# Retention in two transformer layers: one 512-token score triangle against four chunks of 128 with a running state

## The chip, the cores and the metric

One core of a Trainium2 chip runs one program. The metric is the device time of the execution in microseconds. Before the change it is 2685.18 us, median of 3 runs (2685.07 to 2685.32).

## The reference, cut to what matters

The program computes two layers of a three-branch mixer with a feed-forward part, and then one layer of a second kind of block with attention. There are 512 tokens of width 1024, all in float32. The change touches the retention branch of the first two layers, which has 4 heads of 128 dimensions:

```python
log_g = jnp.log(1.0 - 2.0 ** (-5.0 - jnp.arange(h)))
q, k = rotary(q), rotary(k);  q = q * (dk ** -0.5)
def step(state, inp):                       # by chunks of CHUNK tokens
    s = einsum('bhid,bhjd->bhij', qi, ki) * decay_mask     # g^(i-j), i >= j
    intra = einsum('bhij,bhjv->bhiv', s, vi)
    inter = einsum('bhid,bhdv->bhiv', qi * q_decay, state)
    new_state = state * chunk_decay + einsum('bhjd,bhjv->bhdv', ki * k_decay, vi)
    return new_state, intra + inter
y_b = head_norm(out, ret_gn_w, center=True) * silu(rg)
```

Without the chunks this is: output i is the sum over all j up to i of g^(i-j) (q_i . k_j) v_j. Any size of chunk gives the same result.

## The kernel before, in words

Every tensor lies with its channels on the partitions and its 512 tokens along the free dimension; only the values `r_v` have tokens on the partitions, in four tiles of 128. A projection (`pe_block`, lines 504 to 506) multiplies a block of 1024 weight columns with the activations. Weights and activations are split into a high and a low part in a faster format (`w_hi`, `w_lo`), and three products are summed. Weight blocks come by DMA into `raw`; ScalarE makes the high part (line 686), VectorE the low part (line 690), into a ring of four slots. Each engine has its program written out by hand, in one order, and waits on semaphores. The `split(i)` calls stand where block i + 3 is split.

In the stretch around the change TensorE computes the projections GR to GR + 3 (the gates of the other branch), one for each retention head h. Behind projection GR + h stand `ret_scores(h)` (lines 1786 to 1797), `ret_out(h - 1)` (1799 to 1810) and, from h = 2 on, the variance product of a head, `head_var`. The scores are the lower triangle in tiles of 128 keys: key tile 0 with 512 queries, tile 1 with 384, tile 2 with 256, tile 3 with 128, so 1280 columns, in ordinary float32. VectorE multiplies them with the mask g^(i-j) (`ret_decay`, line 2572) into `s_ret`, and TensorE multiplies the values with them, again 1280 columns.

PSUM has eight banks of 512 columns. Banks 0 to 3 take the projections; banks 4 to 7 are given out in a fixed order by `side_banks`. A `Use` of a bank has two semaphores: `filled` (TensorE is done) and `drained` (its reader is done); the next user waits for the one before to be drained. Scores of a head use banks 4, 5 and 6, outputs 7, variances 6.

VectorE's order for head h is: `square_low` (h of 2 and up), the low split of a weight block, `gate_in` (line 2564, projection result times the root), `ret_decay`, `gated` (line 2570). ScalarE's is: the high split of a weight block, `gate_silu` (line 2121), then for the output of the head before a copy, a square and its high part (lines 2070, 2073, 2077), and from h = 2 on a change of the activation table and two steps of the root (lines 2084, 2087).

Of the kernel before, what the change touches and what calls it, by code (L numbers as in the profile page):

```python
# [26 lines left out]
ALU = mybir.AluOpType  # L27
# [17 lines left out]
LEVELS = (1, 128, 64, 32, 16, 8, 4, 2, 256, 512)  # L45
MASKED = LEVELS[1:8]
HALF = P // 2
Q_IN = 6
Q_S = 4
TH = T // 2  # L50
# [55 lines left out]
N_PAR = P_WGA + KD * RANK  # L106

H_FIRST, H_F1POST, H_MPRE, H_MPOST, H_F2PRE, H_F2POST, H_QN, H_KN = 0, 8, 16, 24, 32, 40, 48, 49
N_PAR2 = 50

C_ONES, C_IDENT, C_BD64 = range(3)
N_SQ = 3
# [70 lines left out]
def side_banks():  # L183


    layer = [("pre0", 7), ("tm0", 6), ("ga", 4), ("z0", 7), ("z1", 6)]
    layer += [(key, 4 + i % 4) for i, key in enumerate(k for n in range(len(LEVELS)) for k in level_keys(n))]
    layer += [("out0", 7), ("out1", 7), ("out2", 7), ("var0", 6), ("out3", 7), ("var1", 6), ("var2", 6), ("var3", 6)]
    for h in range(HEADS):
        layer += [(f"s{h}0", 4), (f"s{h}1", 5), (f"s{h}2", 6)]  # L190
        if h >= 1:
            layer += [(f"out{3 + h}", 7)]
        if h >= 2:
            layer += [(f"var{2 + h}", 6)]
    layer += [("out7", 7), ("var6", 6), ("var7", 6), ("post0a", 7), ("post0b", 7), ("pre1", 7), ("post1a", 7), ("post1b", 7)]
    second = [("pre2", 7), ("post2a", 7), ("post2b", 7), ("pre3", 7), ("tm3", 4), ("vt", 4)]
    second += [(f"qvar{i}", 6) for i in range(5)]
    second += [(f"dv{t}", 4 + t) for t in range(TT)]
    second += [(f"pt{u}", 4 + u % 2) for u in range(64)] + [(f"o{g}", 6 + g % 2) for g in range(KD)]
    second += [("post3a", 7), ("post3b", 7), ("pre4", 7), ("post4a", 7), ("post4b", 7)]  # L200
    table, used = {}, [0] * 8
    for key, b in layer:
        table[key] = (b, used[b])
        used[b] += 1
    per = list(used)
    used = [LAYERS * n for n in per]
    for key, b in second:
        table[key] = (b, used[b])
        used[b] += 1
    return table, per  # L210


def build(nc, dram):
    ctx = ExitStack()
    with ctx:
# [35 lines left out]
        row_sum = place("row_sum", [P, 4])  # L251
        row_inv = place("row_inv", [P, 4])
        wait_cell = place("wait_cell", [P, 40])
        ones_r = place("ones_r", [P, P], F32R)
        sq_hi_at = top[0]
        sq_hi = place("sq_hi", [P, 2, T], F32R)
# [44 lines left out]
        s_ret = region("s_ret", [P, 2, 1280], 16)  # L301
# [114 lines left out]
        rot_moved = [sem(f"rot_moved{i}") for i in range(2)]  # L416
        rv_sum = ev("rv_sum", 4)
        rv_cent = ev("rv_cent", 4)
        hn_sq = ev("hn_sq", 8)
        hn_hi = ev("hn_hi", 8)  # L420
        hn_lo = ev("hn_lo", 8)
# [1301 lines left out]
        def _(pe):  # L1723
# [61 lines left out]

            def ret_scores(h, li):
                pe.wait_ge(rot_y.sem, rot_y.upto(li, 4 + h + 1))
                use = side(f"s{h}0", li)
                pe.wait_ge(use.drained, use.n + 1)
                nc.tensor.matmul(use.mem[:, :], r_k[:, h, tok(0)], r_q[:, h, :], start=True, stop=True).then_inc(use.filled, 1)  # L1790
                use = side(f"s{h}1", li)
                pe.wait_ge(use.drained, use.n + 1)
                nc.tensor.matmul(use.mem[:, 0:384], r_k[:, h, tok(1)], r_q[:, h, tok(1, 3)], start=True, stop=True)
                nc.tensor.matmul(use.mem[:, 384:512], r_k[:, h, tok(3)], r_q[:, h, tok(3)], start=True, stop=True).then_inc(use.filled, 1)
                use = side(f"s{h}2", li)
                pe.wait_ge(use.drained, use.n + 1)
                nc.tensor.matmul(use.mem[:, 0:256], r_k[:, h, tok(2)], r_q[:, h, tok(2, 2)], start=True, stop=True).then_inc(use.filled, 1)

            def ret_out(h, li):
                for i in range(3):  # L1800
                    src = side(f"s{h}{i}", li)
                    pe.wait_ge(src.drained, src.n + 2)
                if h == 0:
                    pe.wait_ge(rv_cent.sem, rv_cent.upto(li, 4))
                use = side(f"out{4 + h}", li)
                pe.wait_ge(use.drained, use.n + 1)
                s = s_ret[:, h % 2, :]
                for kt, a, b in ((0, 0, 512), (1, 512, 896), (2, 896, 1152), (3, 1152, 1280)):
                    mm = nc.tensor.matmul(use.mem[:, tok(kt, TT - kt)], r_v[:, kt, tok(h)], s[:, a:b], start=kt == 0, stop=kt == 3)  # L1809
                mm.then_inc(use.filled, 1)  # L1810

            def head_var(n, li):
# [7 lines left out]
            def layer(li):  # L1820
# [38 lines left out]
                pe_values(pe, bl, RV, ou, RV)  # L1859
                for h in range(HEADS):  # L1860
                    project(GR + h)
                    ret_scores(h, li)
                    if h >= 1:
                        ret_out(h - 1, li)
                    if h >= 2:
                        head_var(2 + h, li)
                project(RG)
                ret_out(3, li)
                project(RG + 1)
# [6 lines left out]
                for t in range(GATE_ST):  # L1876
                    o = gate_outs(og, t)
                    for i in range(GATE_BLOCKS):
# [3 lines left out]
                        if i >= O_FIRST:  # L1882
# [4 lines left out]
                            for tile in range(2):  # L1887
                                n = 2 * st + tile
                                if t > 0:
                                    pe.wait_ge(branch_free[n].sem, branch_free[n].upto(li, t))  # L1890
                                else:
                                    src = side((f"s{HEADS - 1}0", f"s{HEADS - 1}1", "var7", "out7")[n], li)
# [169 lines left out]
        def _(act):  # L2062
# [56 lines left out]
            def gate_silu(g, ou, li):  # L2119
                act.wait_ge(drained[ou.bank(GR + g)], ou.uses(GR + g) + 2)  # L2120
                nc.scalar.activation(tgate[g % 2][:, :], tgate[g % 2][:, :], ACT.Silu).then_inc(silu_g.sem, 1)

            def y_high(n, li):

                if n < 4:
# [15 lines left out]
            def layer(li):  # L2141
# [67 lines left out]
                values(bl, RV, ou, RV, r_v, li, 1)  # L2209
                for h in range(HEADS):  # L2210
                    split(GR + h)
                    gate_silu(h, ou, li)
                    if h >= 1:
                        head_copy(3 + h, li)
# [29 lines left out]
                    act.wait_ge(block_done, bg.n(p) + 1)  # L2244
                    nc.scalar.activation(w_hi[:, bg.slot(p), :], gate_weights(bg, li, t, i), ACT.Copy).then_inc(hi_split, 1)

                src = side(f"s{HEADS - 1}2", li)
                act.wait_ge(src.filled, src.n + 1)
                mixed_high(G_T4)
                mixed_high(G_Z)  # L2250
                split(RG)
# [204 lines left out]
        def _(dve):  # L2456
# [115 lines left out]
            def ret_decay(h, li):  # L2572
# [6 lines left out]
                    dve.wait_ge(old.filled, old.n + 1)  # L2579
                use = side(f"s{h}0", li)  # L2580
                dve.wait_ge(use.filled, use.n + 1)
                nc.vector.tensor_tensor(s[:, 0:512], use.mem[:, :], mask, ALU.mult).then_inc(use.drained, 1)
                use = side(f"s{h}1", li)
                dve.wait_ge(use.filled, use.n + 1)
                nc.vector.tensor_tensor(s[:, 512:896], use.mem[:, 0:384], mask[:, 0:384], ALU.mult)
                nc.vector.tensor_tensor(s[:, 1152:1280], use.mem[:, 384:512], mask[:, 0:128], ALU.mult).then_inc(use.drained, 1)
                use = side(f"s{h}2", li)
                dve.wait_ge(use.filled, use.n + 1)
                nc.vector.tensor_tensor(s[:, 896:1152], use.mem[:, 0:256], mask[:, 0:256], ALU.mult).then_inc(use.drained, 1)

            def layer(li):
                bl, ou, s = layer_blocks(li), layer_outs(li), li * 2
# [102 lines left out]
                for h in range(HEADS):  # L2695
                    if h >= 2:
                        square_low(2 + h, li)
                    split(GR + h)
                    gate_in(h, bl, ou, li)
                    ret_decay(h, li)  # L2700
                    gated(h, li)
                    if h == 3:
# [129 lines left out]
                def merged_low(k):  # L2832
                    dve.wait_ge(mg_hi_ev.sem, mg_hi_ev.upto(li, k + 1))
                    nc.vector.tensor_tensor(mg_lo[:, k, :], mg_f[:, k, :], mg_hi[:, k, :].bitcast(F32), ALU.subtract).then_inc(mg_lo_ev.sem, 1)

                square_low(6, li)
                head_norm(5, li)
                mixed_low(G_T4)
# [291 lines left out]
    return v.reshape(-1, P).T  # L3130


def layer_parameters(a):
    out = []
    for li in range(LAYERS):
# [9 lines left out]
def second_gains(a):  # L3145
    cols = [per_partition(a["norm_mix_pre"][0])]
    cols += [per_partition(a[n + "_2"][0]) for n in ("ffn1_post_g", "mix_pre_g", "mix_post_g", "ffn2_pre_g", "ffn2_post_g")]
    cols += [np.concatenate([a[n + "_2"][0][AXIAL]] * 2).reshape(P, 1) for n in ("q_norm_g", "k_norm_g")]
    return np.concatenate(cols, axis=1)


def constants():
# [9 lines left out]
    c = np.arange(T)[None, :] - np.arange(P)[:, None]  # L3162
    log_g = np.log(1.0 - 2.0 ** (-5.0 - np.arange(HEADS)))
    decay = [np.where(c >= 0, np.exp(lg * np.maximum(c, 0)), 0.0).astype(f) for lg in log_g]
    inv = np.power(f(10000.0), -np.arange(HD, dtype=f) / f(HD)).astype(f)

    t = np.arange(T)
# [42 lines left out]
```

## Time and profile before

| | |
|---|---|
| median of 3 runs | 2685.18 us |
| the profiled execution's own time | 2685.19 us |
| its span, from first to last instruction | 2683.4 us |
| TensorE busy | 2668.1 us |
| VectorE busy | 1915.7 us |
| ScalarE busy | 1323.4 us |
| granted TensorE clock, mean | 0.999 |

The busy times overlap. TensorE's products are pipelined: the duration of one reaches past the start of the next, so the distance from start to start, which the chain of waits gives, is what a product costs in a series. The retention of the first layer lies at 224 to 265 us of the span, that of the second at 1082 to 1123 us.

### The profile page before, as it was taken

Reading aid. Unit: us, or ns where it says so; the run is one execution under the profiler, and the core shown is the slowest. Engines: PE = TensorE matmul, PEld = TensorE weight load, DVE = VectorE, ACT = ScalarE, POOL = GpSimd, SP = SyncE. Lnnn points to the kernel's source line nnn. Section 1 sums busy time; section 2 is a strip of 40 time slices with the busy share of each in tenths; the row PEclk is TensorE's granted clock in tenths of the full one; section 3 lists DMA queues with packets and bytes.
Section 4 is the critical chain, followed back from the end, with each engine's and each line's share of the span. In section 5 each row is a group of like instructions: output and inputs, shape, how many; then the busy total and the mean of one; then the engine's idle time right before and its main releaser. Section 6 shows DMA issues by size and latency. Waiting matters only on the chain.

```text
span 2683.4 us, 41896 instructions
## 1 busy us (share of the span) xinstructions
PE 2668.1 (99%) x17044; PEld 2391.4 (89%) x17044; DVE 1915.7 (71%) x2703; ACT 1323.4 (49%) x1984; POOL 57.0 (2%) x59
## 2 busy tenths in 40 slices
PE   9999999999999999999999999999999999999998
PEld 7887999899988888799989998999988877899987
DVE  6946877688854785687678883588854798688843
ACT  5344644555542534554465562455542467455631
POOL 0020000000000003000000000000000000000000
PEclk9999999999999999999999999999999999999999
DMA  4242332333333324133333333233332430233232
GB/s 150 79 126 65 117 102 79 118 118 100 98 108 89 110 83 130 55 118 106 114 100 107 103 93 104 80 118 99 99 107 90 118 107 2 72 118 111 93 103 80
DMA packets 77216, 266.23 MB, mean 99 GB/s; under 512 B 9600, under 2 KB 12032, under 8 KB 76128
## 3 DMA queue, kind: packets, MB, share of 16 engines
q1 hardware_dynamic: 71136, 254.86, 30.6%
q10 hardware_dynamic: 5888, 8.68, 1.2%
q8 instruction: 136, 2.23, 0.3%
q14 instruction: 56, 0.46, 0.1%
HBM read 251.71 MB, written 4.19 MB: 95 GB/s over the span
## 4 chain that ended last, share of the span: by engine, by line
PE 96%; DVE 2%; ACT 1%; issue 0%; DMA 0%; ACTq 0%; DVEq 0%; SPq 0%
PE bank L504 29%; PE bank L505 29%; PE bank L506 29%; PE bank L2035 1%; PE bank L2013 1%; PE bank L1762 1%; PE bank L1999 1%; PE bank L1778 1%; PE bank L1809 1%; DVE w_lo L690 0%; DVE x L856 0%; DVE u_lo L788 0%; ACT w_hi L686 0%; PE bank L1790 0%; DVE ffn_out L847 0%
## 5 line engine op out<-in xcount | busy, mean ns | idle before, releaser
L504 PE MATMUL bank<-u_hi,w_hi 128*128 128x256 f32 (+1 forms) x2352 | 759.1, 323 | 1.6 <-DVE w_lo L690 0.9
L505 PE MATMUL bank<-u_lo,w_hi 128*128 128x256 f32 (+1 forms) x2352 | 749.5, 319 | 0.0
L506 PE MATMUL bank<-u_hi,w_lo 128*128 128x256 f32 (+1 forms) x2352 | 749.2, 319 | 0.0
L690 DVE TENSOR_TENSOR w_lo<-raw,w_hi 128x1024 fp32r<-128x1024 f32 x250 | 311.7, 1250 | 331.4 <-ACT w_hi L686 330.7
L504 PEld LDWEIGHTS bank<-u_hi,w_hi 128*128 128x128 f32 x2352 | 448.2, 191 | 38.5 <-issue 3.9
L505 PEld LDWEIGHTS bank<-u_lo,w_hi 128*128 128x128 f32 x2352 | 448.2, 191 | 32.6 <-issue 2.4
L506 PEld LDWEIGHTS bank<-u_hi,w_lo 128*128 128x128 f32 x2352 | 448.0, 190 | 31.3
L686 ACT ACTIVATE w_hi<-raw 128x1024 fp32r<-128x1024 f32 x250 | 263.3, 1055 | 332.7 <-PE bank L506 257.4
L505 PE MATMUL bank<-cm,w_hi 128*128 128x256 f32 x1152 | 326.0, 283 | 0.0
L506 PE MATMUL bank<-cm,w_lo 128*128 128x256 f32 x1152 | 326.0, 283 | 0.0
L504 PE MATMUL bank<-cm,w_hi 128*128 128x256 f32 x1152 | 326.0, 283 | 0.0
L504 PE MATMUL bank<-hid_hi,w_hi 128*128 128x512 f32 (+1 forms) x792 | 290.2, 366 | 0.0
L505 PE MATMUL bank<-hid_lo,w_hi 128*128 128x512 f32 (+1 forms) x792 | 289.5, 366 | 0.0
L506 PE MATMUL bank<-hid_hi,w_lo 128*128 128x512 f32 (+1 forms) x792 | 289.5, 365 | 0.0
L1024 ACT ACTIVATE w_hi<-rx 128x1024 fp32r<-128x1024 f32 x144 | 153.0, 1062 | 203.2 <-PE bank L506 132.9
L1228 DVE TENSOR_TENSOR w_lo<-rx,w_hi 128x1024 fp32r<-128x1024 f32 x144 | 175.7, 1220 | 81.9 <-ACT w_hi L1024 81.9
L504 PEld LDWEIGHTS bank<-cm,w_hi 128*128 128x128 f32 x1152 | 221.2, 192 | 0.0
L505 PEld LDWEIGHTS bank<-cm,w_hi 128*128 128x128 f32 x1152 | 221.2, 192 | 0.0
L506 PEld LDWEIGHTS bank<-cm,w_lo 128*128 128x128 f32 x1152 | 221.2, 192 | 0.0
L504 PEld LDWEIGHTS bank<-hid_hi,w_hi 128*128 128x128 f32 x792 | 149.4, 189 | 24.2
L505 PEld LDWEIGHTS bank<-hid_lo,w_hi 128*128 128x128 f32 x792 | 149.4, 189 | 24.2
L506 PEld LDWEIGHTS bank<-hid_hi,w_lo 128*128 128x128 f32 x792 | 149.4, 189 | 23.9
(356 smaller groups left out, 4366.2 us busy)
## 6 DMA issues: line engine op xcount, KB each, us to landing
raw<-in_weights SPq DMA_DIRECT2D x314, 512.0 KB, 3.5
rx<-in_weights SPq DMA_DIRECT2D x72, 512.0 KB, 3.5
xr<-in_weights SPq DMA_DIRECT2D x48, 512.0 KB, 3.5
raw<-in_weights SPq DMA_DIRECT2D x32, 384.0 KB, 3.0
rot_s<-rot_in ACTq DMA_DIRECT2D x32, 128.0 KB, 2.4
q_s<-q_in ACTq DMA_DIRECT2D x52, 64.0 KB, 3.1
x<-in_x SPq DMA_DIRECT2D x4, 512.0 KB, 6.5
ret_mask<-in_ret_mask SPq DMA_DIRECT2D x2, 1024.0 KB, 7.4
```

Of the source, the lines that this page charges most:

```text
L504: nc.tensor.matmul(out, st_hi, mv_hi, start=first, stop=False, skip_group_check=onto)
L505: nc.tensor.matmul(out, st_hi, mv_lo, start=False, stop=False, skip_group_check=onto)
L506: return nc.tensor.matmul(out, st_lo, mv_hi, start=False, stop=last, skip_group_check=onto)
L686: nc.scalar.activation(w_hi[:, bl.slot(p), :], raw[:, bl.raw(p), :], ACT.Copy).then_inc(hi_split, 1)
L690: nc.vector.tensor_tensor(w_lo[:, bl.slot(p), :], raw[:, bl.raw(p), :], w_hi[:, bl.slot(p), :].bitcast(F32), ALU.subtract).then_inc(lo_spl ...
L1024: nc.scalar.activation(w_hi[:, bl.slot(p), :], st_weights(bl, f, j, i), ACT.Copy).then_inc(hi_split, 1)
L1228: nc.vector.tensor_tensor(w_lo[:, bl.slot(p), :], st_weights(bl, f, j, i), w_hi[:, bl.slot(p), :].bitcast(F32), ALU.subtract).then_inc(lo_ ...
L1762: mm = nc.tensor.matmul(by_head(bank.mem)[:, :, cols], k[:, i, tok(kt)], by_head(q[:, i, :])[:, :, cols], start=True, stop=True)
L1778: return nc.tensor.matmul(use.mem[:, tok(qt, n)], g_v[:, kt, tok(h)], s, start=first, stop=last)
L1809: mm = nc.tensor.matmul(use.mem[:, tok(kt, TT - kt)], r_v[:, kt, tok(h)], s[:, a:b], start=kt == 0, stop=kt == 3)
L1999: mm = nc.tensor.matmul(ps[ou.bank(E_SCORE + 2 * p + h)][:, :], q[rows, tok(it)], k[rows, :], start=n == 0, stop=n == 2)
L2013: mm = nc.tensor.transpose(use.mem[:, tok(j)], prob[:, u % 4, tok(j)], ident_c)
```

## The change

A head is now computed in four chunks of 128 tokens. Within each chunk the scores of 128 keys and 128 queries are used as before (`s{h}0`, bank 4). For what comes from earlier chunks TensorE first turns the keys of chunks 0 to 2 so that tokens lie on the partitions (`s{h}1`, bank 5); ScalarE copies them out, scaled by a decay for each token (`ret_keys`); TensorE multiplies them with the values, which gives one 128 x 128 product a chunk (`ret_state`, `s{h}2`); VectorE sums these up one after another (`ret_states`), so that state t holds chunks 0 to t. The output is the score product of each chunk and, for chunks 1 to 3, the state times the queries scaled by their decay. The products of `ret_state` go to bank 6 for head 0, and for heads 1 to 3 to bank 5, in which the turned keys stood. Twelve columns of decays join the parameters `par2`; behind the small buffers the next address is rounded up to a multiple of 128 bytes.

```diff
+        top[0] = (top[0] + 127) // 128 * 128
         ones_r = place("ones_r", [P, P], F32R)
...
-        layer += [(f"s{h}0", 4), (f"s{h}1", 5), (f"s{h}2", 6)]
+        layer += [(f"s{h}0", 4), (f"s{h}1", 5)]
...
+        layer += [(f"s{h}2", 6 if h == 0 else 5)]
...
             def ret_scores(h, li):
                 pe.wait_ge(rot_y.sem, rot_y.upto(li, 4 + h + 1))
+                use = side(f"s{h}1", li)
+                pe.wait_ge(use.drained, use.n + 1)
+                for t in range(TT - 1):
+                    mm = nc.tensor.transpose(use.mem[:, tok(t)], r_k[:, h, tok(t)], ident_c)
+                mm.then_inc(use.filled, 1)
                 use = side(f"s{h}0", li)
                 pe.wait_ge(use.drained, use.n + 1)
-                nc.tensor.matmul(use.mem[:, :], r_k[:, h, tok(0)], r_q[:, h, :], start=True, stop=True).then_inc(use.filled, 1)
...
+                for t in range(TT):
+                    mm = nc.tensor.matmul(use.mem[:, tok(t)], r_k[:, h, tok(t)], r_q[:, h, tok(t)], start=True, stop=True)
+                mm.then_inc(use.filled, 1)
+
+            def ret_state(h, li):
+                keys = side(f"s{h}1", li)
+                pe.wait_ge(keys.drained, keys.n + 2)
+                if h == 0:
+                    pe.wait_ge(rv_cent.sem, rv_cent.upto(li, 4))
                 use = side(f"s{h}2", li)
                 pe.wait_ge(use.drained, use.n + 1)
+                for t in range(TT - 1):
+                    mm = nc.tensor.matmul(use.mem[:, tok(t)], ret_kt[:, t, :], r_v[:, t, tok(h)], start=True, stop=True)
+                mm.then_inc(use.filled, 1)
 
             def ret_out(h, li):
-                for i in range(3):
+                for i in (0, 2):
                     src = side(f"s{h}{i}", li)
                     pe.wait_ge(src.drained, src.n + 2)
...
-                for kt, a, b in ((0, 0, 512), (1, 512, 896), (2, 896, 1152), (3, 1152, 1280)):
-                    mm = nc.tensor.matmul(use.mem[:, tok(kt, TT - kt)], r_v[:, kt, tok(h)], s[:, a:b], start=kt == 0, stop=kt == 3)
+                within, later = s_ret[:, h % 2, 0:T], s_ret[:, h % 2, T:]
+                for t in range(TT):
+                    nc.tensor.matmul(use.mem[:, tok(t)], r_v[:, t, tok(h)], within[:, tok(t)], start=t == 0, stop=False)
+                for t in range(TT - 1):
+                    mm = nc.tensor.matmul(use.mem[:, tok(t + 1)], ret_st[:, t, :], later[:, tok(t)], start=False, stop=t == TT - 2)
                 mm.then_inc(use.filled, 1)
... TensorE's order
                 for h in range(HEADS):
                     project(GR + h)
+                    if h == 1:
+                        ret_state(0, li)
                     ret_scores(h, li)
                     if h >= 1:
                         ret_out(h - 1, li)
                     if h >= 2:
                         head_var(2 + h, li)
+                    if h >= 1:
+                        ret_state(h, li)
... ScalarE: new step, and its place
+            def ret_keys(h, li):
+                use = side(f"s{h}1", li)
+                act.wait_ge(use.filled, use.n + 1)
+                for t in range(TT - 1):
+                    decay = par2[:, H_RET + 3 * h + t:H_RET + 3 * h + t + 1]
+                    keys = nc.scalar.activation(ret_kt[:, t, :], use.mem[:, tok(t)], ACT.Copy, scale=decay)
+                keys.then_inc(use.drained, 1)
...
                     split(GR + h)
+                    ret_keys(h, li)
                     gate_silu(h, ou, li)
...
-                src = side(f"s{HEADS - 1}2", li)
-                act.wait_ge(src.filled, src.n + 1)
+                src = side(f"s{HEADS - 1}0", li)
+                act.wait_ge(src.drained, src.n + 2)
                 mixed_high(G_T4)
... VectorE: ret_decay, the sums, and their place
-                nc.vector.tensor_tensor(s[:, 0:512], use.mem[:, :], mask, ALU.mult).then_inc(use.drained, 1)
...
+                nc.vector.tensor_tensor(s[:, T:], r_q[:, h, P:], mask[:, P:], ALU.mult)
...
+                nc.vector.tensor_tensor(tiles[0], tiles[1], within, ALU.mult).then_inc(use.drained, 1)
+
+            def ret_states(h, li):
+                use = side(f"s{h}2", li)
+                dve.wait_ge(use.filled, use.n + 1)
+                nc.vector.tensor_copy(ret_st[:, 0, :], use.mem[:, tok(0)]).then_inc(ret_sum.sem, 1)
+                dve.wait_ge(ret_sum.sem, ret_sum.upto(li, 2 * h + 1))
+                nc.vector.tensor_tensor(ret_st[:, 1, :], use.mem[:, tok(1)], ret_st[:, 0, :], ALU.add).then_inc(ret_sum.sem, 1)
+                dve.wait_ge(ret_sum.sem, ret_sum.upto(li, 2 * h + 2))
+                nc.vector.tensor_tensor(ret_st[:, 2, :], use.mem[:, tok(2)], ret_st[:, 1, :], ALU.add).then_inc(use.drained, 1)
...
                     split(GR + h)
+                    if h >= 2:
+                        ret_states(h - 1, li)
                     gate_in(h, bl, ou, li)
+                    if h == 1:
+                        ret_states(0, li)
                     ret_decay(h, li)
...
+                ret_states(3, li)
                 square_low(6, li)
```

## Rows read from the trace of the kernel before

**Rows 1.** The page: span, TensorE's busy time, the chain's shares by engine.
```profile
span 2683.4 us, 41896 instructions
PE 2668.1 (99%) x17044; PEld 2391.4 (89%) x17044; DVE 1915.7 (71%) x2703; ACT 1323.4 (49%) x1984; POOL 57.0 (2%) x59
PE 96%; DVE 2%; ACT 1%; issue 0%; DMA 0%; ACTq 0%; DVEq 0%; SPq 0%
```

**Rows 2.** Waits of TensorE, whole span: total us, times, longest.
```profile
PE bank L1931 <- POOL warm_r L1696: 1.6, 1, 1.6
PE bank L1999 <- ACT prob L2433: 1.5, 2, 1.3
```

**Rows 3.** Chain of waits, layer 1, behind projection GR + 2: start, us, what.
```profile
242.39 0.86 PE bank L1790 x2
243.25 0.65 PE bank L1793 x2
243.89 0.22 PE bank L1794 x2
244.11 0.43 PE bank L1797 x2
244.55 2.16 PE bank L1809 x8
```

**Rows 4.** Chain of waits, output of gated head 0: eight products of 1280 columns.
```profile
153.28 2.20 PE bank L1778 x16
```

**Rows 5.** Chain of waits, second block's attention: eight float32 transposes of 128 columns.
```profile
2228.11 1.02 PE bank L2013 x8
```

**Rows 6.** Groups by form, VectorE and ScalarE: busy, mean ns, idle before.
```profile
L2586 DVE TENSOR_TENSOR s_ret<-bank,ret_mask 128x128 f32<-128x128 f32 x8 | 2.2, 280 | 0.0
L2443 ACT ACTIVATE prob_t<-bank 128x512 f32<-128x512 f32 x48 | 27.0, 596 | 20.0 <-PE bank L2013 20.0
L1064 ACT ACTIVATE scratch<-bank 128x256 f32<-128x256 f32 x72 | 26.8, 372 | 1.6
```

**Rows 7.** Timeline of TensorE: first score product of heads 1, 2, 3.
```profile
232.42 1.02 PE L1790 MATMUL bank<-r_q,r_k 128*128 128x512 f32 x2
242.23 1.02 PE L1790 MATMUL bank<-r_q,r_k 128*128 128x512 f32 x2
252.49 1.02 PE L1790 MATMUL bank<-r_q,r_k 128*128 128x512 f32 x2
```

**Rows 8.** Timeline of ScalarE: start, us, what, [idle before, releaser].
```profile
236.99 0.60 ACT L2070 ACTIVATE y_b<-bank 128x512 f32<-128x512 f32 x1 [3.02 <-PE bank L1809]
...
246.74 0.60 ACT L2070 ACTIVATE y_b<-bank 128x512 f32<-128x512 f32 x1 [2.96 <-PE bank L1809]
...
252.21 1.28 ACT L2121 ACT_TABLE_LOAD   x1
...
265.10 0.60 ACT L2070 ACTIVATE y_b<-bank 128x512 f32<-128x512 f32 x1 [0.76 <-PE bank L1809]
```

**Rows 9.** Timeline of VectorE around heads 1, 2 and 3.
```profile
232.62 0.69 DVE L2564 TENSOR_TENSOR scratch<-bank,r 128x512 f32<-128x512 f32 x1 [3.10 <-PE bank L506]
...
239.90 1.23 DVE L690 TENSOR_TENSOR w_lo<-raw,w_hi 128x1024 fp32r<-128x1024 f32 x1 [0.26 <-ACT w_hi L686]
...
252.22 1.23 DVE L690 TENSOR_TENSOR w_lo<-raw,w_hi 128x1024 fp32r<-128x1024 f32 x1 [2.83 <-ACT w_hi L686]
253.36 0.68 DVE L2564 TENSOR_TENSOR scratch<-bank,r 128x512 f32<-128x512 f32 x1
```

**Rows 10.** Timeline: a dependent pair on VectorE; a bank freed and TensorE's start.
```profile
277.07 1.22 DVE L2742 TENSOR_TENSOR xr<-raw,xr 128x1024 f32<-128x1024 f32 x1
278.32 1.23 DVE L2744 TENSOR_TENSOR sum_s<-xr,raw 128x1024 f32<-128x1024 f32 x1
...
284.65 0.68 DVE L2564 TENSOR_TENSOR scratch<-bank,r 128x512 f32<-128x512 f32 x1
285.49 0.35 PE L504 MATMUL bank<-u_hi,w_hi 128*128 128x256 f32 x1 [0.29 <-DVE scratch L2564]
```

More of the change, by code:

```diff
@@ L47 @@
 HALF = P // 2
+RET_LATER = T - P
+RET_AT = 2 * P - 1
 Q_IN = 6
@@ L108 @@
 H_FIRST, H_F1POST, H_MPRE, H_MPOST, H_F2PRE, H_F2POST, H_QN, H_KN = 0, 8, 16, 24, 32, 40, 48, 49
-N_PAR2 = 50
+H_RET = 50
+N_PAR2 = H_RET + HEADS * (TT - 1)
 C_ONES, C_IDENT, C_BD64 = range(3)
@@ L300, in build @@
         ret_mask = region("ret_mask", [P, HEADS, T], 36)
-        s_ret = region("s_ret", [P, 2, 1280], 16)
+        s_ret = region("s_ret", [P, 2, T + RET_LATER], 16)
+        ret_kt = region("ret_kt", [P, TT - 1, P], 23)
+        ret_st = region("ret_st", [P, TT - 1, P], 25)
         yc_hi = region("yc_hi", [P, 4, T], 16, F32R)
@@ L418, in build @@
         rv_cent = ev("rv_cent", 4)
+        ret_sum = ev("ret_sum", 2 * HEADS)
         hn_sq = ev("hn_sq", 8)
@@ L1791, in ret_scores @@
[L1791 to L1794, printed above, removed]
+                for t in range(TT):
+                    mm = nc.tensor.matmul(use.mem[:, tok(t)], r_k[:, h, tok(t)], r_q[:, h, tok(t)], start=True, stop=True)
@@ L1795, in ret_scores @@
+                mm.then_inc(use.filled, 1)
[4 more added lines that the diff above has]
+                    pe.wait_ge(rv_cent.sem, rv_cent.upto(li, 4))
                 use = side(f"s{h}2", li)
                 pe.wait_ge(use.drained, use.n + 1)
-                nc.tensor.matmul(use.mem[:, 0:256], r_k[:, h, tok(2)], r_q[:, h, tok(2, 2)], start=True, stop=True).then_inc(use.filled, 1)
+                for t in range(TT - 1):
+                    mm = nc.tensor.matmul(use.mem[:, tok(t)], ret_kt[:, t, :], r_v[:, t, tok(h)], start=True, stop=True)
+                mm.then_inc(use.filled, 1)
@@ L1799, in ret_out @@
             def ret_out(h, li):
-                for i in range(3):
+                for i in (0, 2):
                     src = side(f"s{h}{i}", li)
                     pe.wait_ge(src.drained, src.n + 2)
-                if h == 0:
-                    pe.wait_ge(rv_cent.sem, rv_cent.upto(li, 4))
                 use = side(f"out{4 + h}", li)
                 pe.wait_ge(use.drained, use.n + 1)
-                s = s_ret[:, h % 2, :]
-                for kt, a, b in ((0, 0, 512), (1, 512, 896), (2, 896, 1152), (3, 1152, 1280)):
-                    mm = nc.tensor.matmul(use.mem[:, tok(kt, TT - kt)], r_v[:, kt, tok(h)], s[:, a:b], start=kt == 0, stop=kt == 3)
+                within, later = s_ret[:, h % 2, 0:T], s_ret[:, h % 2, T:]
@@ L1891, in layer @@
                                 else:
-                                    src = side((f"s{HEADS - 1}0", f"s{HEADS - 1}1", "var7", "out7")[n], li)
+                                    src = side((f"s{HEADS - 1}0", f"s{HEADS - 1}2", "var7", "out7")[n], li)
                                     pe.wait_ge(src.drained, src.n + 2)
@@ L2581, in ret_decay @@
                 dve.wait_ge(use.filled, use.n + 1)
-                nc.vector.tensor_tensor(s[:, 0:512], use.mem[:, :], mask, ALU.mult).then_inc(use.drained, 1)
[L2583 to L2586, printed above, removed]
+                nc.vector.tensor_tensor(s[:, T:], r_q[:, h, P:], mask[:, P:], ALU.mult)
+                tiles = [ap.rearrange("p (a n) -> p a n", a=TT) for ap in (s[:, 0:T], use.mem[:, :])]
+                within = mask[:, 0:P].rearrange("p (o n) -> p o n", o=1).to_broadcast([P, TT, P])
+                nc.vector.tensor_tensor(tiles[0], tiles[1], within, ALU.mult).then_inc(use.drained, 1)
+            def ret_states(h, li):
                 use = side(f"s{h}2", li)
                 dve.wait_ge(use.filled, use.n + 1)
-                nc.vector.tensor_tensor(s[:, 896:1152], use.mem[:, 0:256], mask[:, 0:256], ALU.mult).then_inc(use.drained, 1)
+                nc.vector.tensor_copy(ret_st[:, 0, :], use.mem[:, tok(0)]).then_inc(ret_sum.sem, 1)
[3 more added lines that the diff above has]
+                nc.vector.tensor_tensor(ret_st[:, 2, :], use.mem[:, tok(2)], ret_st[:, 1, :], ALU.add).then_inc(use.drained, 1)
             def layer(li):
@@ L3130, in per_partition @@
     return v.reshape(-1, P).T
+RET_LOG = np.log(1.0 - 2.0 ** (-5.0 - np.arange(HEADS)))
 def layer_parameters(a):
@@ L3148, in second_gains @@
     cols += [np.concatenate([a[n + "_2"][0][AXIAL]] * 2).reshape(P, 1) for n in ("q_norm_g", "k_norm_g")]
+    cols += [np.exp(lg * (RET_AT - np.arange(RET_LATER))).astype(np.float32).reshape(TT - 1, P).T for lg in RET_LOG]
     return np.concatenate(cols, axis=1)
@@ L3161, in constants @@
         masks.append(mask[:, np.arange(P) % lev >= lev // 2].astype(f))
-    c = np.arange(T)[None, :] - np.arange(P)[:, None]
-    log_g = np.log(1.0 - 2.0 ** (-5.0 - np.arange(HEADS)))
-    decay = [np.where(c >= 0, np.exp(lg * np.maximum(c, 0)), 0.0).astype(f) for lg in log_g]
+    c = i - j
+    later = np.broadcast_to(np.arange(P, T) - RET_AT, (P, RET_LATER))
+    decay = [np.concatenate([np.where(c >= 0, np.exp(lg * np.maximum(c, 0)), 0.0), np.exp(lg * later)], axis=1).astype(f) for lg in RET_LOG]
     inv = np.power(f(10000.0), -np.arange(HD, dtype=f) / f(HD)).astype(f)
```

## The prediction

> **What bounds the kernel now.** I read the page's busy shares first: TensorE is busy 99% of a span of 2683.4 us, and the chain that ended last is TensorE for 96% of the span [rows 1]. Then all waits of TensorE: the longest entry is 1.6 us, at the start, and the next is 1.5 us in the attention of the second block [rows 2]. So TensorE's queue is the bound nearly everywhere. What shortens its own work shortens the span one for one, and a new wait of TensorE lengthens it one for one. VectorE and ScalarE count only where TensorE comes to wait for them, and that has to be looked for in the few microseconds around each head of the retention, of which there are eight (four heads, two layers).
>
> **TensorE's own work per head.** In the chain of waits the parts of a head's scores take 0.86 + 0.65 + 0.22 + 0.43 = 2.16 us, and its output product takes 2.16 us [rows 3]: 4.32 us for 2 x 1280 columns. The "x2" of each row shows that one float32 product is two passes.
> After the change a head has 4 score products, 3 state products and 7 output products, all of 128 columns: 1792 columns. What does cutting into pieces cost? The output of the gated heads also moves 1280 columns, but in 8 products instead of 4, and takes 2.20 us [rows 4] against 2.16 us [rows 3]: so 0.01 us a product, and 1.65 ns a column. 14 products are then 14 x 0.01 + 1792 x 0.00165 = 3.10 us, or 0.22 us each. The three transposes are priced by the row of eight transposes of the same shape, 1.02 us, so 0.13 us each [rows 5] and 0.38 us for three. Sum 3.48 us, saved 4.32 - 3.48 = 0.84 us a head, **6.7 us in all**. Bounds: if a transpose here cost as much as an ordinary product of its size (0.22 us), three would cost 0.66 and the saving would be 0.56 us a head, 4.5 us in all; if cutting cost nothing (14 x 0.215 = 3.01 us) it would be 0.93 us a head, 7.4 us.
> Rule and row differ here. The Trainium skill, TensorE: Matmul & The Clock Gate, section Terms, has the transposing mode four times as fast for FP32. The row above gives 0.13 against 0.22 us, so only 1.7 times. By that rule three transposes would take 0.16 us instead of 0.38, and the sum over eight heads would be 1.8 us better. I go by the row.
>
> **ScalarE's new work** is three scaled copies of 128 columns out of the bank. The trace has none of that size; 512 columns take 0.60 us and 256 take 0.37 [rows 6], which goes on to about 0.26 us for 128, and at most 0.37. In a row they are under 0.8 us. They stand between the weight split and the sigmoid gate. TensorE needs them only at the state product, which in heads 1 to 3 comes after scores (0.88) and the output product of the head before (1.54), so 2.4 us after the transposes; in head 0 a whole projection lies between. Hidden. The gate's own ScalarE step moves later by about 1 us (in heads 0 and 3 by the table load too, which can then no longer be done while waiting), and VectorE's product with it; both wait for nothing TensorE needs soon. After head 3 ScalarE had 0.76 us to spare when it came to wait for the last output product [rows 8], and the distance from output product to output product grows no shorter by more than it gains: I leave it at nothing.
>
> **VectorE's new work**: the multiplication with the mask falls from 512+384+128+256 to 512+384 columns; three sums of 128 columns come in, 0.28 us each [rows 6], each waiting for the one before. A dependent pair follows with a gap of 0.03 us (277.07 + 1.22 to 278.32) [rows 10]. So from the first one's start to the end of the third 3 x 0.28 + 2 x 0.03 = 0.90 us. TensorE starts 0.15 us after the VectorE instruction that frees its bank has ended (284.65 + 0.68 to 285.49) [rows 10]: 1.05 us in all. The work itself is small. Where it is placed is not.
>
> **The new wait.** The next head's transposes go into bank 5, which the state products of the head before now use too. So TensorE cannot start head h+1 before VectorE has summed head h's states; everything behind it in TensorE's queue, the scores, output and state of that head and the next projection, waits too. For heads 1 and 2 these sums stand in VectorE's queue behind the low split of a weight block (the line 690 instruction), which waits for ScalarE's split of that block, which stands behind ScalarE's work on the head before last.
> Head 3, by the clock of the trace: the output product of head 1 releases ScalarE at 246.74; copy, square, high part, table load, two steps of the root and the weight split follow one another, and the next table load begins at 252.21 [rows 8]; VectorE starts its split at 252.22 and its next instruction at 253.36 [rows 9], 6.62 us after 246.74. TensorE's head 3 began at 252.49 [rows 7], 5.75 us after 246.74. In the new order the state product (3 x 0.22 = 0.66) is added between, so head 3 could begin 6.41 us after that release, while the three sums begin at 6.62 and TensorE resumes at 6.62 + 1.05 = 7.67. **A stall of 1.26 us in each layer, 2.5 us in all.** Bounds: sums of 0.2 us each, 1.0 us; sums of 0.41 us, 1.7 us.
> Head 2: the same chain has no table load and no root; ScalarE is released at 236.99 and VectorE's split of that block starts at 239.90 [rows 8, 9], and occupies 1.14 us, so the sums begin 4.05 us after the release and end with the handover at 5.10. TensorE went from 236.99 to 242.23 [rows 7] in 5.24, and with the state product 5.90. Slack 0.8 us, no stall.
> Head 1: TensorE does the state of head 0 right at the end of the projection (0.66), then transposes (0.38) and scores (0.88), and wants the sums at 1.92. VectorE's gate product starts 0.20 after that point (232.42 to 232.62) [rows 7, 9] and is out of the way at about 0.8; the state's last product ends about 0.2 after its issue, so the sums run from 0.9 to 1.8, and TensorE may go on at 1.95. **0.0 to 0.3 us, taken as 0.1, 0.2 us in both layers.**
>
> **Other edits.** The input of ScalarE's first mixed activations now waits for the end of VectorE's mask product of head 3 instead of the last score product. In ScalarE's queue it stands behind the root of head 5's variance, whose product TensorE issues after scores and output, so later than that; nothing. The 12 more parameter columns move the buffers by 128 bytes, which the rounding keeps on the same remainder: nothing from below or above. The weight stream only comes to be needed a few microseconds sooner; TensorE shows no wait for a transfer [rows 2].
>
> **The sum.** -6.7 + 2.5 + 0.2 = **-4.0 us**. Against the profiled execution's own 2685.19 us (1.8 us of it outside the span) this gives 2681.2; the median before, 2685.18, is the same number. A change of 0.2%, about what a measurement of this kernel can tell from no change, is 5.4 us: my forecast is a gain inside that.
>
> **Rivals.**
> (A) The bank comes free in time. Against it stands the order above, in which the split comes before the sums; for it, that the margin is only 0.2 us on one side and 0.9 us of sums on the other, so if ScalarE's chain got shorter by over 1.2 us (the table load, 1.28 us [rows 8], would do) nothing is left. Then -6.7 + 0.2 = -6.5: **2678.7**.
> (B) Pieces and transposes cost more than the rows of other stages say: the saving is the lower bound of 4.5 us, less 2.7: -1.8, **2683.4**. For it: changing between float32 and the faster format could cost where a state product now stands between the variance product and the projection; against it, in [rows 3] each part costs its columns and no more.
> (C) The end on the other side: ScalarE's scaled copies need another activation table than the gate, so each head pays two table loads, 2 x 1.28 = 2.56 us, in front of the weight split on which the sums hang. Then head 2 stalls 2.56 - 0.8 = 1.8 us and head 3 1.26 + 2.56 = 3.8 us; with head 1's 0.1 this is 5.7 us a layer, and -6.7 + 11.4 = +4.7: **2689.9**. It decides (slower than before) as soon as ScalarE's added delay x has (x - 0.8) + (1.26 + x) + 0.1 over 3.35, that is from x = 1.4 us. Against it: plain copies run in the trace between gate and root steps with no load of their own. The Trainium skill, ScalarE: Activation LUTs, section What ACT_TABLE_LOAD costs, has 1283 ns for the load and some 1380 ns of draining beside it. The trace shows the load and no draining: the load at 252.21 [rows 8] stands right between a weight split and a gate step, and its 1.28 us are all that ScalarE spends on it; by the page's figure this rival would end at some 2700.
>
> **Chances.** Forecast 0.72 (its own range 2679.9 to 2682.6), A 0.14, B 0.09, C 0.05. The range 2678.6 to 2683.5 takes in A's and B's points. Faster by over 0.2% (under 2679.8): A and an edge of the forecast, 0.16. Slower by over 0.2%: part of C, 0.03. Within 0.2%: 0.81.
>
> **What would show it.** TensorE's waits for VectorE's sums: one of about 1 us in each layer in front of the transposes of head 3, little or none at heads 1 and 2. Transposes of 0.13 us, 14 products of 0.22 us a head. ScalarE with as many table loads as before. I am wrong if TensorE shows no wait at head 3 (A), if a head's own work is over 3.7 us (B), or if ScalarE loads tables in front of the key copies (C).

## The result

The changed kernel takes 2690.06 us (median of 20 runs, 2689.65 to 2690.48), the kernel before beside it 2685.32 us: 4.7 us longer, ratio 1.0017 with an interval of 1.0011 to 1.0024. I had forecast 2681.2 us. The profiled execution has a span of 2688.1 us against 2683.4.

The page of the changed kernel, where it answers to [rows 1]:

```profile
span 2688.1 us, 42168 instructions
PE 2670.7 (99%) x17164; PEld 2392.8 (89%) x17164; DVE 1917.2 (71%) x2711; ACT 1329.4 (49%) x2008; POOL 57.0 (2%) x59
```

TensorE is still busy 99% of the span. Its waits in the changed kernel (total us, times, longest), to set against [rows 2]:

```profile
PE bank L1799 <- DVE ret_st L2628: 2.2, 2, 1.1
PE bank L1954 <- POOL warm_r L1704: 1.6, 1, 1.6
PE bank L1836 <- DVE sq_lo L2583: 1.4, 2, 0.7
```

One wait is new, twice 1.1 us, where it was forecast. That explains 2.2 us of loss against a retention that ought to have become 6.7 us shorter. So first, the retention itself: the chain of waits behind projection GR + 2 in the changed kernel, as [rows 3] for the one before (start, us, what).

```profile
241.62 0.33 PE bank L1799 x3
241.94 0.89 PE bank L1804 x8
242.84 0.89 PE bank L1826 x8
243.73 0.69 PE bank L1828 x6
```

Transposes 0.33 us, scores 0.89, output 0.89 + 0.69 = 1.58. The state product is of the same size as the last row, about 0.69, so a head is 3.5 us instead of 4.32, as forecast (3.48). Around head 3 the timelines of VectorE and then of TensorE:

```profile
249.92 1.23 DVE L698 TENSOR_TENSOR w_lo<-raw,w_hi 128x1024 fp32r<-128x1024 f32 x1 [2.83 <-ACT w_hi L694]
251.06 0.28 DVE L2624 COPY ret_st<-bank 128x128 f32<-128x128 f32 x1
251.38 0.29 DVE L2626 TENSOR_TENSOR ret_st<-bank,ret_st 128x128 f32<-128x128 f32 x1
251.70 0.29 DVE L2628 TENSOR_TENSOR ret_st<-bank,ret_st 128x128 f32<-128x128 f32 x1
```

```profile
252.14 0.52 PE L1799 MATMUL bank<-sq_consts,r_k 128*128 128x128 f32 x3 [1.11 <-DVE ret_st L2628]
```

The sums stand behind the low split, exactly as worked out. The changed kernel began the first layer's retention 0.3 us late (225.06 against 224.77). Behind its last output product the next projection starts 1.8 us early, before and then changed:

```profile
264.82 0.48 PE L504 MATMUL bank<-u_hi,w_hi 128*128 128x512 f32 x1
```

```profile
263.05 0.48 PE L512 MATMUL bank<-u_hi,w_hi 128*128 128x512 f32 x1
```

That is 2.1 us gained in one layer, where 6.7 / 2 - 1.26 = 2.1 was forecast. So the loss lies in stages that no line of the change touches. One such stage is the second product of the feed-forward part, whose moving operand is the hidden activation. The timeline of TensorE in the kernel before, first and last of 30 products in a row (start, us, what):

```profile
1699.78 0.39 PE L504 MATMUL bank<-hid_hi,w_hi 128*128 128x512 f32 x1
...
1706.35 0.39 PE L506 MATMUL bank<-hid_hi,w_lo 128*128 128x512 f32 x1
```

and the same kind of row in the changed kernel, the first and last of 30:

```profile
1700.81 0.40 PE L512 MATMUL bank<-hid_hi,w_hi 128*128 128x512 f32 x1
...
1707.56 0.40 PE L514 MATMUL bank<-hid_hi,w_lo 128*128 128x512 f32 x1
```

29 steps take 6.57 us before and 6.75 after: 226.6 against 232.8 ns from start to start. A product's duration on the page is modelled and reaches over the next one, so it isn't the rate, but its mean gives a faint sign of the same (busy us, mean ns, before and changed):

```profile
L504 PE MATMUL bank<-hid_hi,w_hi 128*128 128x512 f32 (+1 forms) x792 | 290.2, 366 | 0.0
L512 PE MATMUL bank<-hid_hi,w_hi 128*128 128x512 f32 (+1 forms) x792 | 293.6, 371 | 0.0
```

From the starts of all products of a kind, without the steps on which TensorE waited:

| moving operand, columns | count | before | changed |
|---|---|---|---|
| hidden, 512 | 1848 | 226.7 ns | 232.4 |
| merged branches, 512 | 288 | 226.7 | 232.4 |
| branch outputs, 512 | 576 | 227.2 | 232.2 |
| mixed activations cm and gm, 256 | 4320 | 120.0 | 118.9 |
| hidden and merged, 256 | 714 | 119.9 | 119.3 |
| activations u, 512 | 2300 | 227.6 | 227.5 |
| activations u, 256 | 4680 | 120.0 | 119.8 |

Every operand with a changed rate lies in the large region; u lies in front of the parameters. Its products of 256 columns changed only among the first eight behind a series on another operand (119.9 to 119.1 ns); from the ninth on they take 120.0 in both kernels. 2712 products of 512 columns lose 5.0 to 5.7 ns, 15.0 us; about 5000 of 256 columns gain 0.6 to 1.2 ns, 5.2 us, and those on u 0.9 us: net +8.9 us. With -6.7 and +2.5 for the retention, the sizes forecast, this is +4.7 us, what was measured.

### The profile page after: what moved, and what is told of

Its sections match the earlier page's. It is cut to its first block, busy times and chain, and to the rows that moved or that the text cites. A ratio compares the mean times of both kernels' runs of the same rounds, so it can differ in the third digit from the quotient of the medians.

```text
span 2688.1 us, 42168 instructions
## 1 busy us (share of the span) xinstructions
PE 2670.7 (99%) x17164; PEld 2392.8 (89%) x17164; DVE 1917.2 (71%) x2711; ACT 1329.4 (49%) x2008; POOL 57.0 (2%) x59
## 4 chain that ended last, share of the span: by engine, by line
PE 96%; DVE 1%; ACT 1%; issue 0%; DMA 0%; ACTq 0%; DVEq 0%; SPq 0%
PE bank L512 30%; PE bank L513 29%; PE bank L514 29%; PE bank L2058 1%; PE bank L2036 1%; PE bank L1770 1%; PE bank L2022 1%; PE bank L1786 1%; DVE w_lo L698 0%; ACT w_hi L694 0%; PE bank L1826 0%; PE bank L1804 0%; PE bank L579 0%; PE bank L587 0%; PE bank L1828 0%
## 5 line engine op out<-in xcount | busy, mean ns | idle before, releaser
L512 PEld LDWEIGHTS bank<-cm,w_hi 128*128 128x128 f32 x1152 | 217.4, 189 | 0.0
L513 PEld LDWEIGHTS bank<-cm,w_hi 128*128 128x128 f32 x1152 | 217.2, 189 | 0.0
```

Source lines behind the costliest of these rows:

```text
L512: nc.tensor.matmul(out, st_hi, mv_hi, start=first, stop=False, skip_group_check=onto)
L513: nc.tensor.matmul(out, st_hi, mv_lo, start=False, stop=False, skip_group_check=onto)
```

## Experiments

The theory P: what counts is where the two operands of a product lie. The twelve parameter columns make `par2` 32 bytes larger, and the rounding behind it puts everything from the ones on 128 bytes higher. Worked out from the order of the `place` calls, weights (address 73856), activations u (16512 + 16384 = 32896) and region (138880) all lie at 128 past a multiple of 256 before; afterwards the region (139008) lies at 0. So its distance to the weights, a multiple of 256 before, is 128 more. The rival, here called C (not the C of the prediction): the longer instruction stream slows TensorE elsewhere.

**b_shift128**, the kernel before with the shift alone:

```diff
+        top[0] += 128
         ones_r = place("ones_r", [P, P], F32R)
```

> The kernel before with nothing changed but 128 bytes left empty in front of the ones (so every later buffer, the large region among them, lies 128 bytes further up). P (placement): products of 512 columns whose moving operand lies in the large region take 232 instead of 227 ns from start to start, products of 256 columns 119 instead of 120; sum of both over their counts about +9 us, so 2694 us. C (the changed instruction stream of TensorE is what slows the other stages): as before, 2685.3 us.

Measured 2694.56 us against 2685.50 (ratio 1.0033, 1.0020 to 1.0046): +9.1 us with no other change. Hidden, 512 columns: 232.4 ns; mixed, 256: 118.8. C falls.

**a_home**, the changed kernel with the shift alone taken back:

```diff
-        wait_cell = place("wait_cell", [P, 40])
+        wait_cell = place("wait_cell", [P, 32])
```

> The changed kernel with the scratch cells 8 columns shorter, which puts the ones and every buffer behind them back on the addresses of the kernel before. P: 512-column products at 227 ns again; what is left is the retention alone, -6.7 us of TensorE's work and +2.2 us of waiting for the sums: about 2681 us. C: 2690 us as with the change.

2681.13 us (ratio 0.9984, 0.9974 to 0.9993). The two halves are now apart: the retention brings -4.4 us against the kernel before beside it (2685.50), the placement costs 8.9. The time is the forecast's to 0.1 us, which is luck in part: the gain was forecast at 4.0 us, and the kernel before took 0.3 us more here than the number from which I started.

**a_front**, a_home with `top = [(nc.sbuf_base + 127) // 128 * 128 + 128]`:

> As a_home, with 128 bytes left empty in front of the first buffer, so that all buffers lie 128 bytes higher and their distances to each other are those of the kernel before. R (the distance between the moving and the stationary operand decides): 227 ns, 2681 us. A (the address of an operand itself decides): every product that is slow with the change stays slow, and those on the activations in front become slow too, over 2692 us.

2681.01 us (0.9974 to 0.9993), all rates as in the kernel before. The addresses themselves, moved by 128 bytes, do nothing; their distances do.

**b_shift256**, as b_shift128 with 256:

> The kernel before with 256 bytes left empty in front of the ones. If the pattern repeats every 256 bytes: 2685.3 us, all products as before. If it repeats at 512 or more: another time, as with 128 bytes, about 2694 us, or worse.

2685.60 us (0.9991 to 1.0010), all rates as before. A distance of 256 bytes is like none, for products of 512 and of 256 columns.

**b_shift64**, as b_shift128 with 64:

> The kernel before with 64 bytes left empty in front of the ones. If only the half of a 256-byte period counts in which two operands lie, 64 bytes stay in the same half: 2685.5 us. If any distance that is no multiple of 256 costs, between 2685.5 and 2694.6 us; if multiples of 128 are a milder case of something worse, over 2694.6 us.

2679.81 us (ratio 0.9980, 0.9970 to 0.9989), **5.4 us faster than the kernel before**. None of the three expectations held. **b_shift192**, as b_shift128 with 192:

> The kernel before with 192 bytes left empty in front of the ones, so the large region lies at 192 of 256 bytes against the weights (64 in b_shift64). If only the size of the distance within the period counts (64 and 192 alike): 2679.8 us with the products' times of b_shift64 (cm 117.9, hidden 512 columns 228.9 ns). If the direction counts: other times, and the products of high times high and high times low parts, which differed in b_shift64, change places.

2671.73 us (ratio 0.9950, 0.9935 to 0.9965), 13.4 us faster than before with one line added. Mean start to start in ns, from the traces, with the region's distance to the weights in 256 bytes:

| | 0 | 64 | 128 | 192 |
|---|---|---|---|---|
| hidden, 512, high x high | 226.8 | 225.9 | 232.5 | 233.4 |
| hidden, 512, low x high | 226.8 | 229.2 | 232.0 | 233.3 |
| hidden, 512, high x low | 226.5 | 231.7 | 232.6 | 233.2 |
| cm, 256, high weights | 120.0 | 117.7 | 118.9 | 114.2 |
| cm, 256, low weights | 120.0 | 118.3 | 118.8 | 113.4 |
| median time, us | 2685.1 to 2685.5 | 2679.8 | 2694.6 | 2671.7 |

The direction counts: 64 and 192 are not alike. The exchange of places between high and low parts, which I had expected with it, did not come for 512 columns: at 192 all three kinds take 233 ns. Products of 512 and of 256 columns want different places. The distance within 256 bytes isn't all that counts: at 64, products of 256 columns on the hidden and merged activations took 113.8 ns, those on cm 117.9. A series of 48 products on cm in the kernel before, first and last, and the same series in b_shift192:

```profile
565.23 0.28 PE L504 MATMUL bank<-cm,w_hi 128*128 128x256 f32 x1
...
570.87 0.28 PE L506 MATMUL bank<-cm,w_lo 128*128 128x256 f32 x1
```

```profile
565.25 0.29 PE L505 MATMUL bank<-cm,w_hi 128*128 128x256 f32 x1
...
570.60 0.28 PE L507 MATMUL bank<-cm,w_lo 128*128 128x256 f32 x1
```

5.64 against 5.35 us over 47 steps: 120.0 against 113.8 ns.

**b_u64**: the activations u moved, weights and region in their old distance.

```diff
-        top = [(nc.sbuf_base + 127) // 128 * 128]
+        top = [(nc.sbuf_base + 127) // 128 * 128 + 64]
...
+        top[0] += 192
         raw = place("raw", [P, RAW, BLK])
```

> The kernel before with x and the activations u 64 bytes further up against weights and large region, which keep their distances (64 bytes in front of x, 192 behind u_lo). If the distance between the two operands is what counts, the 4692 products of 256 columns on u go from 120.2 to about 117 ns and the 2301 of 512 columns from 227.6 to 229: -15.0 + 3.2 = -11.8 us, 2673.5 us, and the products on the large region keep their times. Rival: what counts is the address of the moving operand in the large region only; then nothing changes, 2685.3 us.

2684.98 us (0.9991 to 1.0009): no difference, and yet not the rival's reason. In a series the products of 256 columns on u fell from 120.0 to 117.7 ns; those of 512 columns on u rose from 227.5 to 230 for two of the three kinds; and the values, where u is the stationary and the weights the moving operand, rose from 226.9 to 233.3 ns, a term that I had left out. Summed over all starts, those beside a wait or a change of operand too, this is -9.1 us for 256 columns on u, +5.3 for 512, +3.1 for the values and +0.5 for all the rest: -0.2 us, the time measured. For the values the distance from stationary to moving operand, u to weights, is then 192 of 256, and 233.3 ns is what the hidden activations take at 192. So the rate follows the distance between the two operands also outside the region, whichever of them moves.

Now the wait. **a_home_early**, a_home with the sums ahead of the split:

```diff
                 for h in range(HEADS):
                     if h >= 2:
+                        ret_states(h - 1, li)
                         square_low(2 + h, li)
                     split(GR + h)
-                    if h >= 2:
-                        ret_states(h - 1, li)
```

> a_home with the sums of head h - 1 (h = 2 and 3) placed first in VectorE's order of head h, ahead of the low square and the low split of the weight block. If the position behind the split is what TensorE waits for at head 3: no wait before the transposes, 1.1 us of idle time and 0.15 us of handover less a layer, 2681.1 - 2.5 = 2678.6 us. Rival: the bank comes free early but TensorE then waits for the same chain elsewhere (the state product for the keys, the output for the sums), 2681 us.

2678.46 us (ratio 0.9975, 0.9965 to 0.9984). VectorE sums head 2's states early, and TensorE goes straight from projection to transposes:

```profile
245.25 0.29 DVE L2624 COPY ret_st<-bank 128x128 f32<-128x128 f32 x1 [0.86 <-PE bank L1815]
...
249.61 1.22 DVE L698 TENSOR_TENSOR w_lo<-raw,w_hi 128x1024 fp32r<-128x1024 f32 x1 [2.81 <-ACT w_hi L694]
```

```profile
250.32 0.39 PE L514 MATMUL bank<-u_hi,w_lo 128*128 128x512 f32 x1
250.55 0.49 PE L1799 MATMUL bank<-sq_consts,r_k 128*128 128x128 f32 x3
```

0.23 us from start to start, no idle time. The order on VectorE was the cause of the wait. Its full price was 2.4 us, each run taken against the kernel before beside it (-4.4 and -6.8), or 2.7 between the two medians; 2.5 was forecast.

**a_bank6**, a_home with `layer += [(f"s{h}2", 6)]`, the choice of bank undone:

> a_home with the state products of all heads in bank 6 instead of the turned keys' bank 5. The transposes of head 3 then wait for nothing (-2.5 us), but the state product of heads 2 and 3 stands behind the variance product in bank 6 and waits until ScalarE has read it, after copy, square, high part and a table load, some 3.6 us each: 2681.1 - 2.5 + 4 x 3.6 = 2693 us. Rival: the bank makes no difference beyond the wait at head 3, 2678.6 us.

2702.87 us (ratio 1.0066, 1.0051 to 1.0081), ten more than expected. TensorE's waits:

```profile
PE bank L1815 <- ACT hn_r L2107: 14.7, 4, 3.8
```

Four waits of 3.7 us on average, as expected. What I had not counted is behind them; the stretches of TensorE's work (busy times, then the granted clock) and the state product of head 2:

```profile
248.00:262.00 14.00, 12.31 (x57) 10.34 (x57) 5.21 (x9) 5.91 (x11) 0.00 (x0) 0.79 0.13 39
262.00:276.00 14.00, 11.71 (x55) 10.08 (x56) 6.23 (x9) 7.67 (x11) 0.00 (x0) 0.88 0.07 10
```

```profile
248.17 1.62 PE L1815 MATMUL bank<-r_v,ret_kt 128*128 128x128 f32 x6 [3.54 <-ACT hn_r L2107]
```

The granted clock fell to the lower of its levels, 1.2 GHz, for part of each stretch: the mean of 0.79 over 14 us means 5.9 us at half speed, 0.88 another 3.4, so 9.3 us at half speed, in which the same work takes about 4.6 us more. The second layer shows the same (0.79 and 0.87), and twice 4.6 is 9.3 of the missing 9.9 us. With waits of 1.1 us the clock stayed at 1.00, in a_home's stretch with the same columns:

```profile
222.00:262.00 40.00, 38.88 (x229) 33.86 (x228) 24.05 (x41) 23.82 (x39) 0.00 (x0) 1.00 0.18 53
```

Last, the finding put to use. **a_cm_shift**, **a_cm64** and **a_cm192** are a_home_early with 256 empty bytes in front of the region and only the mixed activations of the feed-forward part (cm), with the raw weight pieces `rx` in front of them, lower than the rest, by 128, 192 and 64 bytes. TensorE doesn't read `rx`. Four conversions of hidden tiles whose bytes they now overlap wait for a later product. The diff of a_cm192, without what it has from a_home_early:

```diff
+        top[0] += 256
         arena = top[0]
...
-        rx = region("rx", [P, 3, BLK], 0)
-        cm = region("cm", [P, 4, 2, KH, TH], 12, F32R)
+        rx = region("rx", [P, 3, BLK], -0.0625)
+        cm = region("cm", [P, 4, 2, KH, TH], 11.9375, F32R)
...
-                elif k in (4, 5):
+                elif k == 4:
                     act.wait_ge(w_sum.sem, w_sum.upto(f, 4 * last + 3))
                 else:
-                    act.wait_ge(block_done, bl.n(p + (1, 2, 4, 6)[(k - 6) // 4]) + (RING + 1))
+                    act.wait_ge(block_done, bl.n(p + (1, 2, 4, 6)[min((k - 5) // 4, 3)]) + (RING + 1))
```

> a_home_early with the region 256 bytes up and, inside it, only the mixed activations cm (moving operands of 3456 products of 256 columns) and the weight pieces in front of them 128 bytes lower than the rest; four conversions of the hidden activations wait for one product later. If the distance of 128 bytes makes 256-column products faster by 1.2 ns (120.0 to 118.8 in b_shift128) and nothing else moves: -4.3 us against a_home_early, 2674.3 us. Rival: the gain belongs to something else in that run, or the later conversions cost as much: no gain.

2673.60 us (ratio 0.9958, 0.9944 to 0.9972); cm at 118.8 ns, hidden 512 still at 226.8.

> a_cm_shift with the mixed activations 192 instead of 128 bytes lower than the rest of the region, that is at +64 of 256 against the weights, where b_shift64 showed 117.9 ns for them instead of 118.8: 3456 x 0.9 ns = -3.1 us more than a_cm_shift, 2670.5 us. Rival: b_shift64's times hang on the whole region's place and not on these operands' own: no better than a_cm_shift, 2673.6 us.

2671.74 us (0.9951, 0.9934 to 0.9968); cm at 117.7 and 118.3 ns, as in b_shift64.

> a_cm_shift with the mixed activations 64 instead of 128 bytes lower than the rest of the region, that is at 192 of 256 bytes against the weights, where b_shift192 showed 114.2 and 113.4 ns for their products (120.0 in the kernel before). If it is their own distance that counts: 2304 x 5.8 + 1152 x 6.6 ns = -21.0 us against a_home_early, 2657.5 us. Rival: the feed-forward part then comes to be bound by VectorE and ScalarE, so that TensorE waits for weight splits: 2660 to 2668 us.

**2655.80 us, ratio 0.9891 (0.9874 to 0.9907)**: 29.6 us below the kernel before and 22.7 below a_home_early, a little more than expected. By the starts in the traces cm's products bring the 21.0 us expected, and those of 256 columns on u, behind cm's series, another 2.3. The same 48 products, the page's busy times, and the three longest waits:

```profile
561.90 0.29 PE L513 MATMUL bank<-cm,w_hi 128*128 128x256 f32 x1
...
567.25 0.28 PE L515 MATMUL bank<-cm,w_lo 128*128 128x256 f32 x1
```

```profile
PE 2637.9 (99%) x17164; PEld 2373.6 (89%) x17164; DVE 1914.6 (72%) x2711; ACT 1332.0 (50%) x2008; POOL 57.0 (2%) x59
```

```profile
PE bank L1955 <- POOL warm_r L1705: 1.6, 1, 1.6
PE bank L2023 <- ACT prob L2467: 1.3, 1, 1.3
PE bank L1837 <- DVE sq_lo L2584: 1.3, 2, 0.7
```

113.8 ns a product over 47 steps, and hidden 512 columns at 226.7: both kinds at a good place at once. TensorE waits hardly more for VectorE than before (3.7 against 3.4 us in all), so the rival (VectorE becomes the bound) did not come.

## Why the prediction was wrong

**The step that failed** is in "Other edits": "The 12 more parameter columns move the buffers by 128 bytes, which the rounding keeps on the same remainder: nothing from below or above." I checked the remainder at 128, the number in the code, and gave the edit a price of exactly nothing although no row of the trace bore on it. b_shift128 prices it at +9.1 us, more than the whole rest of the change (a_home: -4.4) and enough to carry the time out of my range of 2678.6 to 2683.5. It should have been a rival: TensorE is busy for 99% of the span with over 17,000 product instructions, so a third of a nanosecond on each is worth more than all the new waits together.

**Right, by their own rows.** TensorE's work: forecast -6.7 us; a_home_early, in which no new wait is left, gives -6.8. Two small errors cancel in it: transposes cheaper than forecast, pieces a little dearer (3.14 to 3.16 us for the 14 products of a head, forecast 3.10). The stall at head 3: forecast 1.26 us a layer with the handover, measured 1.1 us of idle time and, by a_home_early against a_home, 1.2 to 1.3 us in all. Heads 1 and 2: 0.1 us and none forecast, no wait at either. Pieces: 0.22 us each forecast, 0.89 / 4 = 0.22. The total without the placement: 2681.2 forecast, 2681.1 measured (a_home); as a difference -4.0 forecast, -4.4 measured.

**Right in kind, off in size.** A transpose took 0.11 us from start to start, not 0.13. The Trainium skill, TensorE: Matmul & The Clock Gate, section Terms, has the transposing mode four times as fast for FP32; by the rows here it is twice as fast as an ordinary product of its size (0.11 against 0.22 us). The "x2" of [rows 3] is two instructions; that each is one pass is not shown, and at 1.65 ns a column a float32 product costs 3.7 times the 0.44 ns of one in the split format (226.7 ns for 512 columns). ScalarE's scaled copies took 0.37 us each, my upper bound, and 0.88 us for three in the changed kernel's timeline, where I had said under 0.8:

```profile
252.69 0.88 ACT L2152 ACTIVATE ret_kt<-bank,par 128x128 f32<-128x128 f32 x3 [2.81 <-PE bank L1799]
```

They were hidden, as forecast.

**The rivals.** A (no stall) was wrong as the kernel stood, and is what a_home_early makes. B's price did not come. C (slower through table loads) gave nearly the measured time, by chance: there are as many table loads as before, and its mechanism had nothing to do with it. The side of the result was right in a rival with 0.05, for a wrong reason.

## What to carry over

Where an edit changes the size of a buffer, list the addresses of every tensor that TensorE reads, before and after, against each other and not only against the alignment in the code. Read the rate from start to start of products that the change does not touch: the duration column shows it only faintly. If a change that should help TensorE's own work makes a kernel slower, take the shift back alone first; it costs one run. Where a reader frees a bank, its place in the reader's queue decides: put it ahead of whatever waits for a third engine.

## What the runs showed of the hardware

- The rate of products in the split float32 format depends on the distance between moving and stationary operand along the partition (address of the moving one less that of the stationary one, within 256 bytes). Tried were distances of 0, 64, 128, 192 and 256 bytes; 0 and 256 gave the same. At 192 a product of 256 columns takes 113.4 to 114.2 ns from start to start against 120.0 at 0; one of 512 columns 233.3 against 226.7. At 64 it depends on the operand too: for 256 columns 113.8 (hidden and merged), 117.9 (cm) and 117.7 (u, in b_u64). Moving all buffers together by 128 bytes changed nothing.
- It is not settled why. Writes and reads of VectorE and ScalarE at the same time are not the reason for the 512-column products: with both engines idle those on the hidden activations took 226.7 ns in the kernel before, 232.4 in b_shift128 and 233.3 in b_shift192, and with both busy 227.0, 232.6 and 233.7. Nor is the place of one moving operand against the next, which the shifts of the whole region left as it was. Whether the weights loaded for a product count or those loaded for the next one during it, the runs don't tell apart. Distances between the multiples of 64 were not tried, the mixed activations gm (864 products, 114.2 ns in b_shift192) were not moved alone, and u was not put at 192.
- Waits of 3.5 to 3.8 us on TensorE were followed by a granted clock at 1.2 GHz for part of the next microseconds (0.50 from 248 to 252 us in a_bank6), and this cost some 10 us beside the 14.7 us of the four waits themselves. Waits of 1.1 us did not have this effect.
